# Transposed one-hot gather, skipped gather slots and norm gains kept as a column and a row, in a one-layer RWKV/RG-LRU/MoE step

## What is computed

```
x  = x + merged @ w_out                       # 320 tokens x 1024
t  = rmsnorm(x) * norm2                       # norm2: 1024 gains
g  = top-1 of 4 groups by softmax(t @ router_group + b)
e  = top-2 of the group's 8 experts by softmax(t @ router_expert + b)
x += sum over the two experts of gate * (silu(t @ gate_e) * (t @ up_e)) @ down_e
y  = rmsnorm(x) * final_norm
```

## Time and profile before

| | us |
|---|---|
| median of 3 runs | 816.77 |
| lowest, highest | 816.7, 818.26 |
| the profiled execution | 820.28 |
| its span, first to last instruction | 818.5 |
| TensorE busy | 765.5 (94%) |
| VectorE busy | 426.5 (52%) |
| ScalarE busy | 255.8 (31%) |
| POOL busy | 73.7 (9%) |
| moved by DMA | 162.37 MB, mean 198 GB/s |

### The profile page before, as it was taken

The page is one execution under the profiler, slowest core; times in us unless marked ns, Lnnn a source line. Parts: engine busy times, 40 slices in busy tenths (PEclk is TensorE's granted clock), DMA queues, the critical chain, the costliest instruction groups (busy, mean ns, idle before and its releaser), DMA issues.

```text
span 818.5 us, 18378 instructions
## 1 busy us (share of the span) xinstructions
PE 765.5 (94%) x7164; PEld 476.8 (58%) x7164; DVE 426.5 (52%) x1137; ACT 255.8 (31%) x619; POOL 73.7 (9%) x85
## 2 busy tenths in 40 slices
PE   4999999999999999999999899998899999988884
PEld 4666666666666666666666664454555555544441
DVE  3364677778767867777687746245113211111116
ACT  4224353452443433534524523221111111111112
POOL 3000000400000000000000000001222222212110
PEclk9999999999999999999999989999999999999997
DMA  9553161870251341610703715978999999999975
GB/s 224 128 128 73 28 163 36 156 188 11 61 155 26 82 113 26 158 37 26 188 11 94 300 33 197 385 291 329 312 387 385 387 385 382 391 377 394 392 306 195
DMA packets 117638, 162.37 MB, mean 198 GB/s; under 512 B 27973, under 2 KB 92279, under 8 KB 110920
## 3 DMA queue, kind: packets, MB, share of 16 engines
q1 hardware_dynamic: 100852, 149.14, 54.0%
q0 software_dynamic: 5968, 8.54, 4.3%
q10 hardware_dynamic: 10773, 4.06, 1.9%
HBM read 156.00 MB, written 15.73 MB: 210 GB/s over the span
## 4 chain that ended last, share of the span: by engine, by line
PE 79%; SPq 7%; DMA 6%; ACT 2%; DVE 2%; issue 2%; POOL 0%; ACTq 0%; POOLq 0%; DVEq 0%
PE bank L788 23%; PE bank L1196 9%; PE bank L959 5%; PE bank L1093 4%; PE bank L1203 4%; PE bank L794 4%; PE bank L1037 4%; SPq L552 3%; DMA shared<-in_exp_up 3%; PE bank L1189 3%; SPq L555 2%; PE bank L892 2%; PE bank L760 2%; PE bank L901 2%; SPq L583 1%
## 5 line engine op out<-in xcount | busy, mean ns | idle before, releaser
L788 PE MATMUL bank<-xnT,wall 128*128 128x320 f32 x656 | 196.7, 444 | 2.4 <-ACT vecs L1372 2.4
L788 PEld LDWEIGHTS bank<-xnT,wall 128*128 128x128 f32 x656 | 119.2, 190 | 49.3 <-issue 5.5
L2133 DVE SCALAR_TENSOR_TENSOR vecs<-vecs,bank 128x128 f32<-128x128 f32 x32 | 9.2, 287 | 129.3 <-ACT vecs L1596 126.5
L2129 DVE COPY vecs<-bank 128x512 f32<-128x512 f32 x32 | 22.1, 691 | 58.1 <-PE bank L1203 44.2
L959 PE MATMUL bank<-xnT,wall 128*128 128x320 f32 x128 | 47.9, 456 | 0.3
L1596 ACT ACTIVATE vecs<-bank 128x128 f32<-128x128 f32 x32 | 8.9, 277 | 121.9 <-PE bank L1196 121.9
L1196 PE MATMUL bank<-scratch 128*64 128x256 f32 x320 | 39.8, 405 | 6.6 <-DMA scratch<-in_exp_up 5.4
L1196 PE MATMUL bank<-vecs,scratch 128*64 128x256 f32 x352 | 40.4, 382 | 5.8 <-DMA vecs<-in_exp_up 5.0
L683 POOL DMA_INDIRECT merged<-xn2d,gidx x4 | 3.7, 917 | 416.0 <-DVE gidx L2085 415.1
L1189 PEld LDWEIGHTS bank<-consts_sb,merged 64*128 64x128 f32 x240 | 28.7, 199 | 13.8 <-issue 13.8
L689 POOL DMA_INDIRECT ybuf<-vecs,sidx x30 | 30.4, 1015 | 69.9 <-DVE vecs L2129 69.3
(11 more groups left out here) (420 smaller groups left out, 1359.3 us busy)
## 6 DMA issues: line engine op xcount, KB each, us to landing
wall<-in_w_in SPq DMA_DIRECT2D x58, 512.0 KB, 5.9
vecs<-in_exp_gate SPq DMA_DIRECT2D x11, 1024.0 KB
vecs<-in_exp_up SPq DMA_DIRECT2D x11, 1024.0 KB
scratch<-in_exp_gate SPq DMA_DIRECT2D x10, 1024.0 KB
scratch<-in_exp_up SPq DMA_DIRECT2D x10, 1024.0 KB
scratch<-in_exp_down SPq DMA_DIRECT2D x6, 1024.0 KB
shared<-in_exp_gate SPq DMA_DIRECT2D x10, 512.0 KB
shared<-in_exp_up SPq DMA_DIRECT2D x10, 512.0 KB
```

Source lines behind the costliest of these rows:

```text
L788: q = mm(tpbank(L, name), wbuf[name][:, k, :], xnT[:, k, :], start=(k == 0), stop=(k == KC - 1))
L2129: CP(ye[:, e % 2, :], bank[6 + e % 2][:]).then_inc(S("ye"), 1)
```

## The change

- The one-hot product is made in transposed form: a piece of xn2 with every eighth feature (128 of them) is the stationary operand, disp (128 slots) the moving one. Its result is xgT directly, in two banks of four pieces each. For the folded tile two half products (64 x 64) stand in for one. The copies of rows, the eight transposes and `rows_ps` go. SP now waits for `gT_ps` 2, the end of the second bank.
- xn2 no longer has the gains. norm2 is loaded as a column, `n2` (128 x 8), and each expert's rows get their gains when they leave the bank: for the first two experts by eight scaled copies on ScalarE, for the others by a multiply on VectorE (`gained`), which replaces ScalarE's copy. Expert 0 waits for the first bank only, and for the second halfway through its product.
- The first four gathers skip empty slots too. The clamp goes.
- final_norm is loaded as eight rows of 128 into `murows` at the start. After experts 14 and 16 `final_gains` copies it to all partitions by eight small products, and ScalarE copies them to fnb, and at expert 30 to fnh.
- The big loads of norm2 and final_norm go from SP's queue.

```diff
+        n2 = sb("n2", [P, KC])
-        murows = sb("murows", [NMU + KC, P])
+        NROWS = NMU + 2 * KC
+        murows = sb("murows", [NROWS, P])
...
-            sp.dma_start(norm2b, a["norm2"].broadcast_to([P, D])).then_inc(S("x1_in"), 16)
...
-                sp.dma_start(norm2h[at64(h), :], a["norm2"][:, c].broadcast_to([64, 512])).then_inc(S("x1_in"), 16)
...
-            sp.wait_ge(S("rows_ps"), 2)
+            sp.wait_ge(S("gT_ps"), 2)
...
-            sp.wait_ge(S("gu"), LAST_OF[3] + 1)
-            sp.dma_start(fnb, a["final_norm"].rearrange("(a d) -> a d", a=1).broadcast_to([P, D])).then_inc(S("fn_in"), 16)
-            for h in range(2):
-                src = a["final_norm"].rearrange("(a d) -> a d", a=1)[:, 512 * h:512 * h + 512]
-                sp.dma_start(fnh[at64(h), :], src.broadcast_to([64, 512])).then_inc(S("fn_in"), 16)
...
+            pool.dma_start(n2[:], a["norm2"].rearrange("o (p k) -> p (o k)", k=KC)).then_inc(S("rt_in"), 16)
...
-                    gather(e % 4, gidx[:, e:e + 1], f"xg{e % 4}", N - 1 if e >= ONE_HOT + 4 else None)
+                    gather(e % 4, gidx[:, e:e + 1], f"xg{e % 4}")
...
-            for h in range(2):
-                b, c = bank[3 if h else 0], slice(512 * h, 512 * h + 512)
-                for t in range(2):
-                    mm(b[:], disp[:, t].rearrange("p e s -> p (e s)"), xn2[:, t, c], start=(t == 0), stop=False)
-                mm(b[:], disp[at64(h), 2].rearrange("p e s -> p (e s)"), xn2h[at64(h), :], start=False, stop=True).then_inc(S("rows_ps"), 1)
-            pe.wait_ge(S("rows_c"), 2)
-            for k in range(KC):
-                c = P * (k % 4)
-                q = tr(bank[1 if k < 4 else 4][:, c:c + P], xg01[:, k:D:KC], ident)
-                if k % 4 == 3:
-                    q.then_inc(S("gT_ps"), 1)
+            for g in range(2):
+                b = bank[4 if g else 1]
+                for j in range(4):
+                    for t in range(2):
+                        mm(b[:, P * j:P * j + P], xn2[:, t, 4 * g + j:D:KC], disp[:, t].rearrange("p e s -> p (e s)"),
+                           start=(j == 0 and t == 0), stop=False, skip_group_check=True)
+                for j in range(4):
+                    for h in range(2):
+                        q = mm(b[at64(h), P * j:P * j + P], xn2h[at64(h), 4 * g + j:512:KC],
+                               disp[at64(h), 2].rearrange("p e s -> p (e s)"), start=False, stop=True, skip_group_check=True)
+                q.then_inc(S("gT_ps"), 1)
...
+            def final_gains(part):
+
+                if part:
+                    pe.wait_ge(S("late"), 3)
+                for c in range(4):
+                    r = NMU + KC + 4 * part + c
+                    q = mm(bank[5][:, P * c:P * c + P], ident[0:NROWS, r:r + 1].broadcast_to([NROWS, P]), murows[:], start=True, stop=True)
+                q.then_inc(S("late_ps"), 1)
...
+            act.dma_start(murows[NMU + KC:, :], a["final_norm"].rearrange("(c p) -> c p", p=P)).then_inc(S("st_in"), 16)
...
+            for g in range(2):
+                act.wait_ge(S("gT_ps"), g + 1)
+                for j in range(4):
+                    k = 4 * g + j
+                    q = A(xgT[:, 0:2, k, :], bank[4 if g else 1][:, P * j:P * j + P].rearrange("p (b s) -> p b s", b=2), ACT.Copy, scale=n2[:, k:k + 1])
+                q.then_inc(S("gT"), 1)
...
-                if 2 <= e < NE - 1:
-                    next_cols(e + 1)
...
+                if e in (14, 16):
+                    part = (e - 14) // 2
+                    act.wait_ge(S("late_ps"), 3 + part)
+                    A(fnb[:, 512 * part:512 * part + 512], bank[5][:], ACT.Copy).then_inc(S("late"), 1)
+                if e == NE - 2:
+                    act.wait_ge(S("late"), 4)
+                    for h in range(2):
+                        A(fnh[at64(h), :], fnb[at64(h), 512 * h:512 * h + 512], ACT.Copy).then_inc(S("late"), 1)
...
+                TS(dst, x, rowst[:, 6 + t:7 + t], None, MUL).then_inc(S("xn2"), 1)
...
-            step(TS(tokf[:, ONE_HOT:ONE_HOT + 4], tokf[:, ONE_HOT:ONE_HOT + 4], N - 1.0, None, MIN))
...
+            def gained(bank_cols, e):
+
+                dve.wait_ge(S("gT_ps"), e + 1)
+                TT(xgT[:, e % 2], bank_cols.rearrange("p (k s) -> p k s", k=KC), n2[:, :, None].broadcast_to([P, KC, CAP]), MUL).then_inc(S("gT"), 1)
...
+                if 1 <= e < NE - 1:
+                    gained(bank[(e + 1) % 2][:], e + 1)
```

More of the change, by code:

```diff
@@ L679, in _, with gather @@
             pool.wait_ge(S("xn2d"), 64)
[L681 to L686, removed]
+            def gather(j, e, sem):
+                pool.indirect_dma_start(xg[j], None, xn2d, bass.IndirectOffsetOnAxis(ap=e, axis=0), bounds_check=N - 1,
+                                        oob_is_err=False).then_inc(S(sem), 16)
             def scatter(b, e):
@@ L719, in _ @@
                     carry(13)
-                    gather(0, gidxo[:, 0:1], "xg0", N - 1)
+                    gather(0, gidxo[:, 0:1], "xg0")
                     pool.wait_ge(S("ye"), j + (NE + 1))
@@ L746, in states @@
             def states():
-                pe.wait_ge(S("st_in"), 16 * 6)
+                pe.wait_ge(S("st_in"), 16 * 7)
                 for c in range(KC):
@@ L753, in states @@
                     tr(bank[1][0:w, 8 * c:8 * c + 8], shrows[:, c * P:c * P + w], ident[0:8, 0:8])
-                tr(bank[2][:, 256:256 + NMU + KC], murows[:], ident[0:NMU + KC, 0:NMU + KC]).then_inc(S("vecT"), 1)
+                tr(bank[2][:, 256:256 + NMU + KC], murows[0:NMU + KC, :], ident[0:NMU + KC, 0:NMU + KC]).then_inc(S("vecT"), 1)
             pe.wait_ge(S("xnT"), 6)
@@ L1190, in T, with GU @@
                 return q
-            def GU(b, xT, w):
+            def GU(b, xT, w, upper=None):
                 for k in range(KC):
+                    if upper and k == KC // 2:
+                        upper()
                     for f in range(2):
@@ L1218, in up, with upper_in @@
                 landed(e, "g")
-                pe.wait_ge(S("gT"), max(e + 1, ONE_HOT))
+                pe.wait_ge(S("gT"), e + 1)
                 if e >= 2:
                     pe.wait_ge(S("h"), e - 1)
-                GU(bank[2 + e % 2], xgT[:, e % 2], buf(e)).then_inc(S("gu"), 1)
+                GU(bank[2 + e % 2], xgT[:, e % 2], buf(e), upper_in if e == 0 else None).then_inc(S("gu"), 1)
+            def upper_in():
+                pe.wait_ge(S("gT"), 2)
             def turn_rows(e):
@@ L1249, in slot_rows @@
                 else:
-                    pe.wait_ge(S("slotT"), 1)
+                    pe.wait_ge(S("late"), 1)
                     for x in range(ON_CHIP):
                         q = tr(bank[5][:, 64 * x:64 * x + 64], dup[0:64, 2, x, :], ident[0:64, 0:64])
-                q.then_inc(S("slotT_ps"), 1)
+                q.then_inc(S("late_ps"), 1)
[5 more added lines that the diff above has]
+                    q = mm(bank[5][:, P * c:P * c + P], ident[0:NROWS, r:r + 1].broadcast_to([NROWS, P]), murows[:], start=True, stop=True)
+                q.then_inc(S("late_ps"), 1)
             def hot_out(x):
@@ L1282, in _ @@
                     slot_rows(e // 2 - 5)
+                if e == 14:
+                    pe.wait_ge(S("late"), 2)
+                    final_gains(0)
+                if e == 16:
+                    final_gains(1)
             dn(NE - 1)
-            pe.wait_ge(S("slotT"), 2)
+            pe.wait_ge(S("late"), 4)
             hot_out(0)
@@ L1608, in _ @@
                 with act.Fori(0, NOV) as j:
-                    act.wait_ge(S("gT_ps"), j + (NE + 1))
-                    A(xgT[:, 0], bank[7][:].rearrange("p (k s) -> p k s", k=KC), ACT.Copy).then_inc(S("gT"), 1)
                     act.wait_ge(S("gu"), j + (NE + 1))
@@ L2008, in _ @@
                 inverse(t)
-                scale(t, norm2h if t == 2 else norm2b, "xn2")
+                plain(t)
             dve.wait_ge(S("lg_ps"), 2)
@@ L2116, in slot_columns @@
             def slot_columns(part):
-                dve.wait_ge(S("slotT_ps"), part + 1)
+                dve.wait_ge(S("late_ps"), part + 1)
                 if part == 0:
-                    CP(late[:, 0:512], bank[5][:]).then_inc(S("slotT"), 1)
+                    CP(late[:, 0:512], bank[5][:]).then_inc(S("late"), 1)
                 else:
-                    CP(late[:, 512:640], bank[5][:, 0:128]).then_inc(S("slotT"), 1)
+                    CP(late[:, 512:640], bank[5][:, 0:128]).then_inc(S("late"), 1)
             def outputs(e):
@@ L2150, in _ @@
                 with dve.Fori(0, NOV) as j:
+                    dve.wait_ge(S("gT_ps"), j + (NE + 1))
+                    TT(xgT[:, 0], bank[7][:].rearrange("p (k s) -> p k s", k=KC), n2[:, :, None].broadcast_to([P, KC, CAP]), MUL).then_inc(S("gT"), 1)
                     dve.wait_ge(S("th"), j + (NE + 1))
@@ L2175, in _ @@
                 q.then_inc(S("x2r"), 1)
-            dve.wait_ge(S("fn_in"), 48)
+            dve.wait_ge(S("late"), 6)
```

36 lines of the change are left out of this document (10 added, 26 removed).

## The result

| | before | after |
|---|---|---|
| median of 10 runs each, us | 817.43 | 813.38 |
| lowest, highest | 816.63, 821.89 | 811.92, 816.56 |
| ratio, 95% interval | | 0.995 (0.9933 to 0.9968) |
| the profiled execution | 820.28 | 813.49 |
| its span | 818.5 | 811.7 |

The change makes the kernel 4.05 us faster (2.6 to 5.5 by the interval). The forecast was 6.4, and the time lies in its range.

A forecast was written before the change was run, and what follows sets the result against it. The prediction took the expert weight stream on the DMA engines as the bound. Restart -0.2, gathers -4.7 and tail -1.5 gave -6.4: 813.9 us for the profiled execution, 810.4 for the median, range 807.6 to 815.1.

The forecast's parts named there:

- part 1: Transposed one-hot product: 0.23 us a full product, end at 557.8, weight stream restarting 0.2 us earlier.
- restart: SP's next weight loads after the one-hot product: 0.2 us earlier, bounds 0.5 earlier to 1.4 later.
- gathers: First four gathers, empty slots skipped: stream 4.7 us shorter, bounds 1.9 to 6.0.
- part 2: Skipped slots in the first four gathers: 1.9 us for bytes and 2.8 for lost rate, 4.7 together.
- tail: After the weight stream: last scatter lands in 4.7 us without broadcasts beside it, 1.5 us gained, bounds 0 to 2.7.
- part 5: final_norm's 0.75 MB of broadcasts leave the queue's end: 1.5 us gained; its small products and copies cost 0.
- SP's pause for expert 2: SP issues nothing from 574.24 to 582.86, awaiting expert 2's buffer; stream expected to stay fed, with 9 us reserve.
- the slower rival: One-hot product's loads stall on the eight-element step: 0.6 us a product, 8.4 late, 819.0 in all; chance 0.04.
- point of decision: Price of a one-hot product from which the slower rival decides: 0.5 us, 6.2 us late.
- loss per gathered row: Stream time lost to gathered rows beyond bytes: 0.014 us a row from a later gather, 0.016 in the four.
- Part 3: Gain and 512-column copy moved to VectorE in the expert loop: about 0.69 us of work, cost 0 under idle time.
- Part 4: norm2's 0.75 MB of broadcasts leave SP's queue: worth 0; new tiny loads at the start cost 0 to 0.3 us.

The follow-up runs named there:

- e5: Kernel before plus one unused tensor of 32 bytes a partition, which moves the buffers behind it: 810.2 us, ratio 0.9908.
- e3: Kernel before with only the skipping of empty slots in the first four gathers: 814.62 us, ratio 0.9972.
- e2: Changed kernel with the transposed one-hot product undone (rows, copies, eight transposes back), the rest kept: 807.08 us, ratio 0.9879.
- e1: Changed kernel with stationary pieces of neighbouring features instead of every eighth (first two experts compute wrong values): 809.02 us, ratio 0.99.
- e4: Changed kernel with the clamp back, so the first four gathers write all 64 slots again: 816.77 us, ratio 0.9987.
- e8: Changed kernel with the 0.75 MB of final_norm broadcasts back at the end of SP's queue, into an unread buffer: 813.1 us, ratio 0.9945.
- e6: Changed kernel with n2 allocated behind all buffers, so the others have their old offsets: 820.0 us, ratio 1.0026.

## Why the prediction came out as it did

The runs add up. From the kernel before, the pad gives -7.2 (e5), the skip -3.3 (e3), and part 1 +6.3 (e2 to the changed kernel): -4.2, where -4.05 was measured. e2 says it without part 1: it holds all the rest of the change and is 10.8 under the kernel before in its rounds, where pad and skip give 10.5. For the work of parts 3, 4 and 5 nothing is left over, as far as intervals of 1 to 2 us to each side of a term can tell.

| term | forecast | measured | by |
|---|---|---|---|
| restart (part 1) | -0.2 | +4.4, +6.3 with the open rest (ratios: +4.1, +5.8) | e1, e2 |
| gathers (part 2) | -4.7 | -3.3, -3.4 (ratios: -2.3, -3.0) | e3, e4 |
| tail (part 5) | -1.5 | 0 (0.7 in the profiles) | e8 |
| parts 3 and 4, their work | 0 | 0 | remainder |
| place of the buffers | not seen | -6.6 to -7.2 | e6, e5 |
| sum | -6.4 | -4.05 | |

**What bounds the kernel** was right: everything that moved the time did it through the weight stream, its restart or its rate, and a faster stream showed in full. SP's pause for expert 2 is still there, and the stream stayed fed through it.

**Part 1 failed at its first step, the price of a product.** The prediction took 0.23 us from the earlier trace rows, rows whose weights are neighbours in memory. The new loads step over eight elements, and the price is 0.51 (0.48 within a group). It had this as the slower rival, at 0.6, and set it aside since the transposes in the earlier trace rows carry the same step. That was one row for another form of instruction. The mechanism was this rival's, and the price reached its point of decision, 0.5. The delay did not: the restart came 4.4 us later and not 6.2, since the rival charged the half products alike and they stayed cheap. The kernel would still have become slower, as e6 shows with 2.1 to 2.6 us, but for the shift, and that is because parts 2 and 5 gave less than their 6.2. Sixteen products cost 8.1 us where 3.7 was forecast. The half products went nearly as forecast, 2.5 for all sixteen against 2.1. The gain in order of work behind the product (no copies, no transposes ahead of expert 0) is real, expert 0 starting as the product ends where it waited 2.7, and it is worth nothing, as the prediction had it.

**Part 2 was right in kind and too large.** The skip spares more than bytes, and the rate between 572 and 586 came out at 352, above the 350 that was named. The mis-sized term is the loss per gathered row: a quarter microsecond of a later gather gave 0.014 us a row and the stretch itself 0.016, the runs 1.7 to 2.3 us / 176 = 0.010 to 0.013. The four landings did not fall to 7 us either: 8.05 for the first, and for the fourth this, where it had 14.8:

```profile
merged<-xn2d,gidx POOLq DMA_INDIRECT x1, 10.8
```

Expert 2 started 2 us later than the 573 that was named, which cost nothing:

```profile
575.18 5.36 PE L1188 MATMUL bank<-scratch 128*64 128x256 f32 x32 [0.90 <-issue]
...
580.58 0.34 SPq L552 DMA_DIRECT2D scratch<-in_exp_gate  x1
```

SP's next load at 580.58 found the engines still full.

**Part 5 had the scatter right and its worth wrong.** The scatter did speed up, to 5.00 us, under the 5.5 that was named. But the prediction counted that as time with the step behind it unchanged, and there the reads of ybuf took 1.5 longer. The stage from expert 30's product to the end is 35.2 before and 35.5 after. e2, without the transposed product, has 34.5, but e5, which keeps the broadcasts, has 34.5 too, so that is no sign of part 5 either.

**Part 3's cost of nothing** fits the remainder, though one of its readings was off: the 58.1 us in the earlier trace rows are all idle time ahead of the output copy, and 44.2 of them end with TensorE.

**Part 4 was put at nothing for its work, and its 32 bytes were the largest term of all.** No view of the trace of before shows this, for it holds one placement only. What it did show, and I read as a fact of the stream, was a rate of 384 GB/s in the one loop and nothing to compare it with.

So the forecast came near by luck, through errors that cancel: part 1 too cheap by 4.6 to 6.5, the gathers and the tail too hopeful by 1.4 and 1.5, and against them a gain of 6.6 to 7.2 that was not in the sum.

## What to carry to other kernels

Where a stream of transfers bounds a kernel, look at the byte address of its destination buffers first, and put small tensors where they don't move the big ones; compare the stream's rate in two profiles before giving a change the credit for it. Don't let a float32 product load its stationary operand with a step of eight elements when a queue waits for it: here that cost the queue 4.4 us. A sign of success, as a transfer that lands sooner, is no gain until the stage around it is shorter.

## What was not expected of the hardware

- Weight transfers run at 394 to 397 GB/s in the kernels that have most of their buffers at 0 modulo 128 bytes (and modulo 256), and at 384 to 386 in those that have them at 32, 64 or 96 modulo 128.
- A weight load of a float32 product, 128 x 128, takes 192 ns with neighbouring elements, 196 with a step of two and 335 with a step of eight, and the product goes from 0.26 to 0.51 us.
- The final reads of 2.62 MB end 10.8 to 11.1 us after the scatter in every kernel with the transposed product, which lies 240 us ahead of them, and 9.0 to 10.2 in the others but one, which has 11.8.
